# First panel behind three layer norms multiplied on columns that are not yet normalised, and the low weight half taken last in panels done output by output

## The reference, cut to what matters

```
p = h @ w_in                                   # ca, cb, rq, rk, ... from one projection
x = layer_norm(ALPHA*x + gate1 * mixer(p) @ w_out, ln1)
h = x * (1 + scale2) + shift2                  # then the feed forward
p = causal_conv3(h @ w_up) ; a, v = split(p)
x = layer_norm(ALPHA*x + gate2 * (silu(a) * v) @ w_down, ln2)
```

## Time and profile before

| | us |
|---|---|
| median of 3 runs (range) | 3418.07 (3417.81 to 3419.47) |
| the profiled execution's own time | 3417.27 |
| its span, first to last instruction | 3415.5 |
| PE busy | 3297.4 (97%) |
| DVE busy | 2102.7 (62%) |
| ACT busy | 1321.9 (39%) |
| PE matmul, panels in block two: start to start | 0.227 |

### The profile page before, as it was taken

One profiled execution on the slowest core, in us unless ns is written; L12 is line 12 of the kernel. 1 busy time (PEld: TensorE's weight loads), 2 busy tenths in 40 slices (PEclk: granted clock), 3 DMA queues, 4 the chain that ended last, 5 costly groups with the idle time before them and its releaser, 6 DMA issues. The chain is left out here.

```text
span 3415.5 us, 39169 instructions
## 1 busy us (share of the span) xinstructions
PE 3297.4 (97%) x15472; PEld 2651.3 (78%) x15472; DVE 2102.7 (62%) x2693; ACT 1321.9 (39%) x1720; POOL 615.9 (18%) x496
## 2 busy tenths in 40 slices
PE   8899999999999999999999999999999999999998
PEld 6577788886677788877788777888777887778886
DVE  8854576548753666447866746554677666465545
ACT  4664322234663322234333234343444332343323
POOL 2222232131212222111000232000210001320002
PEclk9999999999999999999999999999999999999999
DMA  3122454322122544332212232222221212222222
GB/s 131 43 64 81 176 199 189 128 93 78 38 76 88 197 189 189 107 121 74 74 62 67 88 105 88 99 99 99 74 87 63 74 59 92 96 87 92 94 98 74
DMA packets 72183, 344.47 MB, mean 101 GB/s; under 512 B 25152, under 2 KB 26048, under 8 KB 35648
## 3 DMA queue, kind: packets, MB, share of 16 engines
q1 hardware_dynamic: 70416, 339.12, 28.8%
q0 software_dynamic: 576, 2.33, 0.2%
q10 hardware_dynamic: 1008, 0.51, 0.1%
HBM read 340.51 MB, written 2.10 MB: 100 GB/s over the span
## 5 line engine op out<-in xcount | busy, mean ns | idle before, releaser
L901 PE MATMUL bank<-Hhi_b,whi_b 128*128 128x512 f32 x2976 | 1205.4, 405 | 42.9 <-ACT Hhi_b L1282 15.5
L902 PE MATMUL bank<-Hhi_b,wlo_b 128*128 128x512 f32 x2976 | 1164.6, 391 | 0.0
L908 PE MATMUL bank<-Hlo_b,whi_b 128*128 128x512 f32 x2976 | 1156.9, 392 | 1.1 <-DVE Hlo_b L2336 0.9
L879 DVE TENSOR_TENSOR wlo_b<-raw_b,whi_b 128x2048 fp32r<-128x2048 f32 (+2 forms) x290 | 624.5, 2153 | 460.8 <-ACT whi_b L873 460.8
L901 PEld LDWEIGHTS bank<-Hhi_b,whi_b 128*128 128x128 f32 x2976 | 562.4, 189 | 186.7 <-issue 30.9
L908 PEld LDWEIGHTS bank<-Hlo_b,whi_b 128*128 128x128 f32 x2976 | 561.2, 189 | 123.0 <-DVE Hlo_b L2336 3.8
L902 PEld LDWEIGHTS bank<-Hhi_b,wlo_b 128*128 128x128 f32 x2976 | 562.4, 189 | 120.1 <-issue 9.1
L873 ACT ACTIVATE whi_b<-raw_b 128x2048 fp32r<-128x2048 f32 (+2 forms) x290 | 511.8, 1765 | 365.0 <-PE bank L908 361.4
L901 PE MATMUL bank<-Uhi_b,whi_b 128*128 128x512 f32 x1024 | 404.9, 395 | 3.7 <-POOL Ulo_b L990 3.7
L902 PE MATMUL bank<-Uhi_b,wlo_b 128*128 128x512 f32 x1024 | 399.8, 390 | 0.0
L908 PE MATMUL bank<-Ulo_b,whi_b 128*128 128x512 f32 x1024 | 386.2, 390 | 0.0
(11 more groups left out here) (253 smaller groups left out, 3397.2 us busy)
## 6 DMA issues: line engine op xcount, KB each, us to landing
raw_b<-in_w SPq DMA_DIRECT2D x234, 1024.0 KB, 4.8
ada_b<-in_wada SPq DMA_DIRECT2D x48, 1024.0 KB, 6.9
raw_b<-in_w SPq DMA_DIRECT2D x40, 512.0 KB, 3.7
raw_b<-in_w SPq DMA_DIRECT2D x16, 768.0 KB, 4.3
rel_b<-in_rel SPq DMA_DIRECT2D x128, 24.0 KB, 2.4
X_keep<-in_x SPq DMA_DIRECT2D x4, 512.0 KB, 9.5
decay_b<-in_decay POOLq DMA_DIRECT2D x2, 1024.0 KB, 6.8
out<-X_keep SPq DMA_DIRECT2D x8, 256.0 KB, 2.0
```

The lines of the kernel that those rows point to most:

```text
L879: self.nc.vector.tensor_tensor(self.wlo[n % RAW_SLOTS][:, 0:words], self.raw[n % RAW_SLOTS][:, 0:words], self.whi[n % HI_SLOTS][:, 0:words ...
L901: self.nc.tensor.matmul(out, whi[:, k, cols], xhi, start=(k == 0), stop=False)
L902: self.nc.tensor.matmul(out, wlo[:, k, cols], xhi, start=False, stop=False)
L908: mm = self.nc.tensor.matmul(out, whi[:, k, cols], xlo, start=False, stop=(k == nk - 1))
```

## The change

1. `products` waits for `whi` alone at first. In panels done output by output, the wlo·xhi matmuls of a piece are collected and issued after all its others, and only they wait for `wlo`. This holds in both blocks.
2. At N1, N2 and N3 the next panel's first product is taken out of its place. ACT and DVE write `Hhi`/`Hlo` of A*x for the columns before they are normalised (items `scaled`), PE adds up the weights' column sums with A and B (32 matmuls of 4 columns), and issues the panel's 48 matmuls between its sums and spreads. Panel n is split between evictions 5 and 6, the one behind it in `lnend`.
3. The normalised columns are still made, for the panels behind. The two outputs are corrected afterwards in their banks (items `unfold`: two DVE passes and one ACT pass each), and only then taken out. This comes behind the second panel, which is now `k_outer`. The first output sits in a small bank, the second in one of the three.

```diff
-            s.product(n, 8, 256, [(i, ("fg", l, c)) for i, c in enumerate(cs)], ("H", l, "ffn"), k_outer=(u0 + j == 0))
+            ahead = halfway is not None and u0 + j == 0
+
+            def gates():
...
+            if not ahead:
+                s.product(n, 8, 256, [(i, ("fg", l, c)) for i, c in enumerate(cs)], ("H", l, "ffn"),
+                          k_outer=(u0 + j == 0))
...
-            for c in cs:
...
+            if not ahead:
+                gates()
...
-            s.product(n, 8, 256, [(i, ("fu", l, c)) for i, c in enumerate(cs)], ("H", l, "ffn"))
+            s.product(n, 8, 256, [(i, ("fu", l, c)) for i, c in enumerate(cs)], ("H", l, "ffn"), k_outer=ahead)
             n += 1
             between()
+            if ahead:
+                norm_outputs(s, l, "mix")
+                gates()
...
-            if i == 0:
+            if i == 0 and l > 0:
+                lead_then = [(job, then) for _, job in cols]
+            elif i == 0 or i == 1 and l > 0:
                 s.product(n, nk, 256, cols, rhs, k_outer=True)
+                if i == 1:
+                    norm_outputs(s, l - 1, "ffn")
+                    for job, lead in lead_then:
+                        lead(job)
...
+        if (l, w) in FOLDED:
+            s.small.take(("sw", l, w))
+            s.small.take(FOLDED[l, w][1][0])
...
+    folded = (l, w) in FOLDED
     if c == 5:
         s.add("lnshift", l, w, 6)
         s.add("lnshift", l, w, 7)
-    if c == 6:
+        if folded:
+            s.round_next()
+    if folded:
+        for i in {4: (0, 1, 4), 5: (2, 3, 5), 6: (6,), 7: (7,)}.get(c, ()):
+            s.add("scaled", l, w, i)
+        if c == 5:
+            s.rest_next()
+    elif c == 6:
         s.split_ahead(n)
...
+FOLDED = {(0, "mix"): ((0, "ffn"), (("fg", 0, 0), ("fg", 0, 1))),
+          (0, "ffn"): ((1, "mix"), (("z", 1, "ca", 0), ("z", 1, "cb", 0))),
+          (1, "mix"): ((1, "ffn"), (("fg", 1, 0), ("fg", 1, 1)))}
+FOLD_ORDER = (0, 1, 4, 2, 3, 5, 6, 7)
+
+
+def layer_norm_stages(s, n, l, w):
+
+    if (l, w) not in FOLDED:
+        s.add("lnend", l, w, None)
+        for k in range(DC):
+            s.add("lnx", l, w, k, None)
+        return
+    after, jobs = FOLDED[l, w]
+    s.load_ahead(n)
+    s.wide.take(jobs[1])
+    s.last_use[n] = jobs[1]
+    s.round_next()
+    s.add("lnend", l, w, n)
+    s.rest_next()
     for k in range(DC):
+        s.temp("hf", 2, ("hf", *after, k))
         s.add("lnx", l, w, k, after)
+        if k > 0:
             s.add("lnlo", *after, k - 1)
+    s.add("lnlo", *after, DC - 1)
+
+
+def norm_outputs(s, l, w):
+
+    for i in range(2):
+        s.temp("hf", 2, ("hf", "norm", l, w, i))
+        s.add("unfold", l, w, i)
...
+        k_outer = len(pieces) > 1 and pieces[0][0] == pieces[1][0]
...
-        if ("w", n) not in seen:
-            seen.add(("w", n))
+        if ("whi", n) not in seen:
+            seen.add(("whi", n))
             pe.wait_ge(*self.steps.after("whi", n))
+        for _, stretch in itertools.groupby(pieces, key=lambda p: None if k_outer else p[1]):
+            low = []
+            for k, group in itertools.groupby(stretch, key=lambda p: p[0]):
+                group = list(group)
+                xhi, xlo, hi_ready, lo_ready = self.operand(rhs, k)
+                if hi_ready not in seen:
+                    seen.add(hi_ready)
+                    pe.wait_ge(*self.steps.after(*hi_ready))
+                for _, cc, job in group:
+                    if k == 0:
+                        self.reuse(pe, job)
+                    out, cols = self.bank[self.s.bank(job)][:], slice(cc * P, (cc + 1) * P)
+                    self.nc.tensor.matmul(out, whi[:, k, cols], xhi, start=(k == 0), stop=False)
+                    low.append((out, wlo[:, k, cols], xhi, k, job))
+                if k_outer:
+                    self.low_products(pe, seen, n, low)
+                    low = []
+                if lo_ready not in seen:
+                    seen.add(lo_ready)
+                    pe.wait_ge(*self.steps.after(*lo_ready))
+                for _, cc, job in group:
+                    out, cols = self.bank[self.s.bank(job)][:], slice(cc * P, (cc + 1) * P)
+                    mm = self.nc.tensor.matmul(out, whi[:, k, cols], xlo, start=False, stop=(k_outer and k == nk - 1))
+                    if k_outer and k == nk - 1:
+                        mm.then_inc(*self.steps.mark("pe", job))
+            self.low_products(pe, seen, n, low, nk - 1)
+
+    def low_products(self, pe, seen, n, low, last=None):
+
+        if low and ("wlo", n) not in seen:
+            seen.add(("wlo", n))
             pe.wait_ge(*self.steps.after("wlo", n))
...
+        for out, w, x, k, job in low:
+            ends = k == last
+            mm = self.nc.tensor.matmul(out, w, x, start=False, stop=ends)
+            if ends:
+                mm.then_inc(*self.steps.mark("pe", job))
...
+                l, w = a[:2]
                 pool.wait_ge(*after("ms", l, w))
                 for c in range(1, DC - 1):
+                    if (l, w) in FOLDED:
+                        pool.wait_ge(*after("sc", l, w, c))
                     ng.tensor_tensor(X[:, c], X[:, c], msb[:], ALU.subtract).then_inc(*mark("pool", ("xm", l, w, c)))
...
+            elif kind == "scaled":
+                l, w, c = a
+                act.wait_ge(*after("xc", l, w, c))
+                act_e.activation(k.Hhi[:, c], X[:, c], ACT.Copy, scale=normed(l, w, 0, c))\
+                    .then_inc(*mark("act", ("sc hi", l, w, c)))
+            elif kind == "unfold":
+                l, w, i = a
+                job = FOLDED[l, w][1][i]
+                z = k.out_of(job)[:]
+                act.wait_ge(*after("rooted", *job))
+                act_e.activation(z, z, ACT.Identity, bias=wsum[:, i, 1:2]).then_inc(*mark("act", ("normed", *job)))
...
+                    act.wait_ge(*after("sc free", l, w, c))
...
+            elif kind == "scaled":
+                l, w, c = a
+                dve.wait_ge(*after("sc hi", l, w, c))
+                nv.scalar_tensor_tensor(out=k.Hlo[:, c], in0=X[:, c], scalar=normed(l, w, 0, c),
+                                        in1=k.Hhi[:, c].bitcast(F32), op0=ALU.mult, op1=ALU.subtract)\
+                    .then_inc(*mark("dve", ("sc", l, w, c)))
...
+            elif kind == "unfold":
+                l, w, i = a
+                job = FOLDED[l, w][1][i]
+                z = k.out_of(job)[:]
...
+                dve.wait_ge(*after(*job))
...
+                nv.scalar_tensor_tensor(out=buf(u), in0=msb[:], scalar=wsum[:, i, 0:1], in1=z, op0=ALU.mult,
+                                        op1=ALU.subtract).then_inc(*mark("dve", ("centred", *job)))
+                dve.wait_ge(*after("centred", *job))
+                names = [("rooted", *job), ("free", u)] + ([("free", ("br", l, w))] if i == 1 else [])
+                nv.scalar_tensor_tensor(out=z, in0=buf(u), scalar=-1.0, in1=k.out_of(("br", l, w))[:], op0=ALU.mult,
+                                        op1=ALU.mult).then_inc(*mark("dve", *names))
...
+    def column_sums(pe, l, w, n):
+
+        j, sw, (whi, wlo) = NORMS[l, w][0], ("sw", l, w), k.weights(n, 256)
...
+        for i in range(2):
+            cols, out = slice(i * P, (i + 1) * P), k.out_of(sw)[:, 4 * i:4 * i + 4]
+            for c in range(DC):
+                nt.matmul(out, whi[:, c, cols], few_coef[:, j, c], start=(c == 0), stop=False)
+                mm = nt.matmul(out, wlo[:, c, cols], few_coef[:, j, c], start=False, stop=(c == DC - 1))
+
+    def scaled_products(pe, l, w, n, columns):
+
+        jobs, (whi, wlo) = FOLDED[l, w][1], k.weights(n, 256)
+        for c in columns:
+            first, last = c == FOLD_ORDER[0], c == FOLD_ORDER[-1]
+            pe.wait_ge(*after("sc", l, w, c))
+            for i, job in enumerate(jobs):
...
+                nt.matmul(out, whi[:, c, cols], k.Hhi[:, c], start=first, stop=False)
+                nt.matmul(out, wlo[:, c, cols], k.Hhi[:, c], start=False, stop=False)
+                mm = nt.matmul(out, whi[:, c, cols], k.Hlo[:, c], start=False, stop=last)
+                names = ([("sc free", l, w, c)] if i == 1 else []) + ([job] if last else [])
...
+                if n is not None:
+                    column_sums(pe, l, w, n)
...
+                if n is not None:
+                    scaled_products(pe, l, w, n, FOLD_ORDER[0:1])
...
                 spread(("bm", l, w), few_mean).then_inc(*mark("pe", ("bm", l, w)))
+                if n is not None:
+                    scaled_products(pe, l, w, n, FOLD_ORDER[1:3])
...
                 spread(("br", l, w), few_var).then_inc(*mark("pe", ("br", l, w)))
+                if n is not None:
+                    scaled_products(pe, l, w, n, FOLD_ORDER[3:])
```

More of the change, by code:

```diff
@@ L891, in products @@
-        for k, group in itertools.groupby(pieces, key=lambda p: p[0]):
-            group = list(group)
-            xhi, xlo, hi_ready, lo_ready = self.operand(rhs, k)
```

(55 more changed lines are left out.)

43 lines of the change are left out of this document (22 added, 21 removed).

## The result

The changed kernel takes 3468.1 us (median of 4 runs, 3464.1 to 3469.3) against 3417.9 us for the kernel before on the same chip: 1.0141 times its time, 95% interval 1.0129 to 1.0154. That is 50 us more, where 24 were forecast, and outside the range. The profiled execution has a span of 3465.6 us.

What follows compares the result with a forecast made beforehand. PE, busy for 97% of the span, bounds the kernel by its work and the waits between. Norms 22.6 + contention 3.0 + clock 5.1 - low half last 6.7 = +24.0 on 3417.27: 3441 us; 8-in-10 range 3424 to 3457.

Steps and rivals of the forecast that it cites:

- The low half last: Panels outside the norms: low matmuls issued last cover most waits for `wlo`, -6.7 us in sum.
- The seven waits of the prediction: PE's waits for a late `wlo` outside the norms, from 0.36 to 1.62 us each, put at 7.2 us together.
- The late `wlo` that I priced at 0.4: The 1.35 us wait: DVE comes later by 12 small coefficient instructions added once, so about 0.4 stays.
- Scaled columns and contention: Scaled `Hlo` on DVE slowed beside POOL's adds: 0.5 for two of six, 1 us a norm, +3.
- the walk: Step-by-step dating of DVE, ACT and PE at N1 with the trace's durations; N1, N2, N3 sum to +22.6 us.
- The idle of 4.7 us inside the last panel: At N1 PE stands before column 6's sums until its square; the 9 matmuls behind start at 2080.7 instead of 2075.97.
- lies in PE's slack mostly: Low clock after each norm's earlier idle is mostly hidden; only the later one is paid, 3 x 1.7 = +5.1 us.
- Column sums 3.5: At each folded norm, 32 short matmuls on PE at 0.11 us each take 3.5 us.
- dearer short matmuls: Rival, 15%: column sums take 7.3 us, +11, and the idle inside the panel drags the clock down: 3452 to 3458.
- The chain, 13.1: From "normalise 0" to the last `hf`: 13.8 us before, 12.0 at ACT's pace, taken as 13.1 with POOL further ahead.
- The bank: Third panel's first output waits for its bank behind the correction: +9.0 at N1, +6.3 at N2, +7.3 at N3.
- The sum: Whole kernel: 22.6 for the norms + 3.0 contention + 5.1 clock - 6.7 low half last = +24.0 us.

Runs made afterwards that it cites:

- e12: Changed kernel with columns 2, 3, 5 scaled behind eviction 6, column sums late, outputs corrected inside the last columns' chain and held in the statistics' banks: 3443.0 us.
- e5: Changed kernel with idle products keeping PE busy through its waits at the three folded norms: 3454.7 us, 1.0113.
- e6: Changed kernel with the banks of the two folded outputs swapped: 3459.4 us, 1.0126.
- e8: Changed kernel with the third panel's low split placed behind the correction and gates: 3459.9 us, 1.0122.
- all four: Changed kernel with columns 2, 3, 5 scaled behind eviction 6, late column sums, swapped output banks and the third panel's low split behind the gates: 3448.0 us, 1.0086.

## Why the prediction was wrong

Direction and places were right, the size wasn't.

- *The low half last, -6.7*: measured alone -6.7, with an interval of 3 to 9 us. (The seven waits of the prediction add up to 7.1 us, not 7.2; its 6.7 is 7.1 less 0.4.) Where it goes back (1644) I had not seen; that it stays beside the fold isn't shown. The late `wlo` that I priced at 0.4 was 1.14.
- *Scaled columns and contention, +1 us a norm*: six `Hlo` took 6.7 us instead of 4.2, 2.5 too much, and eviction 6 came 2.0 later than in the walk. The means hide how. Taken one by one, the six took 0.75, 1.78, 0.74 and 1.26, 1.75, 0.74 us, so three were long and three weren't; these are two of the long ones, with POOL's sum between them:

```profile
2077.99 1.26 DVE L2410 SCALAR_TENSOR_TENSOR Hlo_b<-X_keep,coef_b,Hhi_b 128x512 fp32r<-128x512 f32 x1 [1.14 <-ACT Hhi_b L2126]
2078.67 1.71 POOL L1952 TENSOR_TENSOR qa_b<-qa_b,sq_b 128x512 f32<-128x512 f32 x1
2079.18 1.75 DVE L2410 SCALAR_TENSOR_TENSOR Hlo_b<-X_keep,coef_b,Hhi_b 128x512 fp32r<-128x512 f32 x1
```

Each long one ends some 0.55 us behind the end of the POOL instruction that it met: 2079.26 behind 2078.71, 2080.93 behind 2080.38, 2070.65 behind 2070.09. And POOL's sum took 1.71 instead of the 1.27 of the one ahead of it; it in turn had started while the first of them ran. In e12 four at 2087.68, just after POOL's last sum had ended at 2087.21, took 2.74, 0.69 each. The Trainium skill, "SBUF: State Buffer", section "Who interferes with whom", has the later instruction blocked altogether; the trace agrees. What it did not come to is blocking throughout, with all six slowed: three of six met a sum of POOL, at 0.5, 1.0 and 1.0 us, where the forecast had two at 0.5.

- *The idle of 4.7 us inside the last panel*: there, 5.6 us in three pieces. **The step that failed is the sentence behind it, that the low clock it brings "lies in PE's slack mostly".** PE has no slack from there to the mean's spread: the last 9 matmuls, eviction 7, the column sums, the last sums and the spread are one chain. In 16 us at 0.74 it lost 4 us. Against the walk's dates eviction 6 is 2.0 late, eviction 7 4.0, the last sums 4.7, "normalise 0" 6.0 (of that 0.6 is DVE's split ahead of it, 2.87 beside POOL and not 2.28). The 2.0 between the two evictions are the clock's: e5 has 4.3 us there. For the whole norm e5 gives the clock's share as 3.3 to 3.8 us a norm, the later dip included, against 1.7.
- *Column sums 3.5*: 4.0, of them 0.5 from five at the low clock. The rival "dearer short matmuls" had the nearest time, 3452 to 3458, but not by its first term: they took 4.0 and not 7.3. Its other one, a clock dragged down, held, but for the most part ahead of them and behind them. That a stretch at the low clock also follows them (last section) stood nowhere in the forecast.
- *The chain, 13.1*: 13.9, as before the change. POOL's lead gave nothing.
- *The bank*: 9.7, 7.0 and 9.8 us of waiting, as foreseen (6 to 10). From "normalise 0" to the third panel the walk had 26.8, the trace 27.0.
- *The sum*: behind the norms 47.3 instead of 30.7, and N2 isn't cheap: 13.5 against 9.0 with contention and clock. There the last panel's matmuls are fewer, so PE waits longest of all for POOL's sum of the columns (3.90 us), which the walk had left out.

In short, the walk was right in DVE's order and wrong in taking PE for an engine with time to spare where DVE holds it up.

## What to carry to other kernels

When work is added to the engine that feeds a chain, its price isn't its length: 4.9 us of VectorE's time cost 7 to 8 a norm, since three of the seven instructions met one of GpSimd and took 2.5 us more, and since the stops that they caused also brought TensorE's clock to its lower level under the next links of the chain. Before calling a low clock hidden, follow who waits for the matmuls that run under it. And when a buffer's wait is mended (e6, e8 to e12), look for what holds the engine one step earlier: sums of single edits came to 28 us, all four to 20.
